# Attention weights transposed by a DMA on Sync's queue instead of by TensorE and ScalarE copies, in a two-layer hybrid decoder trunk on eight cores

## The chip, the cores and the metric

The kernel runs on the 8 NeuronCores of one Trainium2 chip. Each core has TensorE (matmuls), VectorE, ScalarE, GpSimd and SyncE, which run side by side and wait for each other on semaphores, and 16 DMA engines that all queues share. Every core computes one of the 8 sequences of the batch by itself, with the same program and the same weights; the cores exchange nothing. The metric is the device time of the slowest core in microseconds (us).

## The reference

Two layers over x of shape (8, 2048, 1024). What matters, cut down:

```python
h = rmsnorm(x, norm_mix_pre); z = h @ w_in             # u|v (gMLP), q|k|v, pool channels, 3 gates
ya, yc = gmlp_branch(...), pool_branch(...)
# differential attention, causal, 4 heads, two components of 64 each, v of 128:
sc = einsum('bqhcd,bkhcd->bhcqk', q, k) * 64**-0.5     # masked with -inf above the diagonal
p = softmax(sc)                                        # both components c = 0, 1
w = p[:, :, 0] - lam * p[:, :, 1]
out = einsum('bhqk,bkhe->bqhe', w.astype(v.dtype), v)
yb = rmsnorm(out, subln_g) * (1 - lambda_init)
merged = sum(sigmoid(gate_i) * (y_i @ w_branch_i)); x = x + rmsnorm(merged @ w_out)
x = x + rmsnorm(swiglu(rmsnorm(x)))                    # D_FF = 2816
```

The product of w with v needs w with the keys on the partitions, while the softmax leaves the queries there. So each block of 128 queries by 128 keys has to be transposed once. That transposition is what is changed.

## The kernel before

**Stages.** The work is cut into four stages: (layer 0, first half of the tokens), (layer 0, second half), (layer 1, first half), (layer 1, second half), 1024 tokens each. A stage projects K, V and Q, then runs its attention mixed in between dense matmuls: the feed-forward part of the stage before (from stage 1 on), the gMLP and pool projections, and the gates and branches `G`/`B`. Last come the 16 merge groups of branch 1 (attention's own: a gate group `ps<-HB,WS` of 8 matmuls and a branch group `ps<-QY,WS` of 4), and the output projection. Stage numbers below are 0 to 3.

**Attention's units.** One unit `u` is one head of one block of 128 queries: 32 units in a stage, `qb = u // 4` the query block, `h = u % 4` the head. A unit of an even stage has `qb + 1` = 1 to 8 key blocks, one of an odd stage `8 + qb + 1` = 9 to 16; over the four stages that is 128 units and 1088 blocks of 128x128. The keys are taken in chunks of up to 1024, so a unit of an odd stage has two chunks. For each chunk: `qk` (the score products of both components, matmuls of 64 rows, into four PSUM banks; on the last chunk the mask is added), `max` on VectorE, `exp` on ScalarE into `PB[:, u % 2, comp]`. After the last chunk: `w` (sums, reciprocals, lambda) and `wk` on VectorE, which combines the components in pieces of 512 columns, in place, into `PB[:, u % 2, 0]`. Then, in pieces of four blocks: `tr`, matmuls against the identity that put the transposed weights into a PSUM bank; `wt`, ScalarE's copy of that bank into `WT[:, rnd % 2]`; `pv`, matmuls of `WT` with `V` that accumulate into the output's bank. When the fourth head of a query block is done, `oc`, `f`, `y`, `yt`, `ye` normalize and transpose its output, and the next block's first `pv` waits for `y`. `PB` has two places: ScalarE's `exp` of unit u waits until the last `tr` of unit u - 2 has read its place.

**What sets the order.** Nothing is scheduled at run time. The class `Order` plays the program through with planned durations and writes down one fixed order for each engine; the engines then run those lists, each strictly in order. `dense` places a dense group and before it calls `run_events`, which places attention's steps (`attention_step`) if what they need is, by the plan, there. A step of `qk` also waits for its share of the dense work (`targets`). What is left of a stage's attention after the fourth merge group is placed by `finish_attention`, with no dense work in between, because the fifth group needs the last query block. The plan reckons a DMA at `mb / GBPS` plus 2.0 us, one after the other through one `dma_free` for all queues.

**Sync's queue** carries the residual loads (`xo`: 2 MB, 1.5 MB and twice 0.25 MB at each stage's merge; `xr`, 256 KB each through `NXR` places), the stores and the final output. Weights are loaded by GpSimd's queue into four slots `WS`.

## Time and profile before

| | |
|---|---|
| median of 3 runs | 2515.87 us (2510.47 to 2516.42) |
| the profiled execution's own time | 2516.2 us |
| span of its slowest core (core 0) | 2514.7 us; the cores have 2495.1 to 2514.7 us |
| mean granted TensorE clock, core 0 | 0.961 of full |
| TensorE busy (core 0) | 2289.6 us, 91% of the span |
| VectorE / ScalarE busy | 1453.5 us (58%) / 1275.8 us (51%) |
| 16 DMA engines: GpSimd's queue / Sync's queue | 38.0% / 9.6% of their time |

All rows are of core 0, the slowest. Times count from the start of its span. A busy TensorE is not TensorE at its peak, because matmuls overlap: a group's busy time divided by its count is more than one matmul costs in a run of them. PEclk is the granted clock as a share of full (1.0 is 2.4 GHz, 0.5 is 1.2 GHz).

### The profile page before, as it was taken

What the parts mean: (1) busy time and instruction counts of PE and PEld (TensorE: products, weight loads), DVE (VectorE), ACT (ScalarE), POOL (GpSimd) and SP (SyncE); (2) the same over time, 40 slices, a digit from 0 to 9 for tenths busy, and PEclk for the clock granted to TensorE, in tenths of its full rate; (3) what the DMA queues carried; (4) which work ended last, traced back from release to release, by engine and by line L of the source; (5) the groups of instructions that cost most, each with busy time, mean ns of one, the idle gap of its engine ahead of it and who ended that gap; (6) DMA issues with size and microseconds to landing.
All of it is one profiled execution on the core that took longest, in us unless ns stands there. A gap on an engine that the chain in (4) does not pass through costs nothing.

```text
span 2514.7 us, 39549 instructions; the slowest of 8 cores (2495.1 to 2514.7 us)
## 1 busy us (share of the span) xinstructions
PE 2289.6 (91%) x12332; PEld 1078.9 (43%) x12568; DVE 1453.5 (58%) x2618; ACT 1275.8 (51%) x2728; POOL 289.4 (12%) x573
## 2 busy tenths in 40 slices
PE   5999689999998997999998999999999899888996
PEld 2444344444443443444444444444444444333442
DVE  2467626777657884545524754567765778364313
ACT  2556635555675663634445542645667566442122
POOL 1111000000111100011011210001111111100011
PEclk9999789999998997999999999999999999889998
DMA  8433337333344442644346346643334533865458
GB/s 193 66 51 58 86 59 159 59 57 54 59 83 134 69 85 61 150 87 68 60 64 150 80 64 150 136 70 60 55 53 71 153 58 51 172 138 99 78 73 199
DMA packets 83369, 230.87 MB, mean 92 GB/s; under 512 B 8288, under 2 KB 9056, under 8 KB 82144
## 3 DMA queue, kind: packets, MB, share of 16 engines
q0 software_dynamic: 49456, 150.43, 38.0%
q1 hardware_dynamic: 33712, 77.91, 9.6%
q8 instruction: 108, 1.77, 0.3%
q14 instruction: 93, 0.76, 0.1%
HBM read 345.16 MB, written 33.55 MB: 151 GB/s over the span
## 4 chain that ended last, share of the span: by engine, by line
PE 81%; DMA 6%; DVE 5%; issue 4%; ACT 3%; POOL 0%; SPq 0%; another core or an unknown queue 0%; DVEq 0%; ACTq 0%; POOLq 0%
PE ps L1039 57%; PE ps L1080 11%; DMA WS<-wblk 4%; PE ps L1201 3%; PE ps L1130 2%; PE ps L1230 2%; PE ps L1215 2%; DVE st L1521 1%; DVE R L1425 1%; DMA R<-xT 1%; DVE R L1422 1%; PE ps L1205 1%; DVE TM L1425 1%; ACT WT L1283 1%; PE ps L1145 1%
## 5 line engine op out<-in xcount | busy, mean ns | idle before, releaser
L1039 PE MATMUL ps<-HB,WS 128*128 128x512 bf16 x4987 | 1165.7, 384 | 42.6 <-DMA WS<-wblk 19.8
L1039 PEld LDWEIGHTS ps<-HB,WS 128*128 128x128 bf16 x5120 | 493.2, 99 | 626.1 <-issue 88.7
L1283 ACT ACTIVATE TG<-ps 128x512 f32<-128x512 f32 x368 | 219.6, 597 | 526.2 <-PE ps L1039 518.7
L1521 DVE TENSOR_REDUCE st<-ps 128x1 f32<-128x1024 f32 (+7 forms) x384 | 343.2, 907 | 154.7 <-PE ps L1205 139.5
L1346 ACT ACTIVATE PB<-ps,st 128x1024 bf16<-128x1024 f32 (+7 forms) x384 | 331.2, 865 | 139.8 <-DVE st L1521 122.3
L1425 DVE SCALAR_TENSOR_TENSOR TM<-TG,ps 128x512 f32<-128x512 f32 x304 | 208.4, 686 | 321.1 <-PE ps L1039 169.9
L913 POOL DMA_DIRECT2D WS<-wblk x334 | 181.6, 544 | 1821.7 <-PE ps L1039 1472.0
L1080 PE MATMUL ps<-R,WS 128*128 128x512 bf16 x1371 | 313.2, 379 | 6.8 <-DMA WS<-wblk 2.9
L1283 ACT ACTIVATE R<-ps 128x512 f32<-128x512 f32 (+1 forms) x256 | 149.3, 596 | 230.9 <-PE ps L1080 108.9
L1039 PE MATMUL ps<-R,WS 128*128 128x512 bf16 x988 | 240.3, 381 | 6.6 <-DVE R L1422 1.9
L1425 DVE SCALAR_TENSOR_TENSOR PB<-PB,st 128x512 bf16<-128x512 bf16 (+3 forms) x320 | 204.4, 665 | 3.6
L1080 PEld LDWEIGHTS ps<-R,WS 128*128 128x128 bf16 x1408 | 133.7, 98 | 160.7 <-issue 13.4
L1039 PE MATMUL ps<-WS,HB 128*128 128x512 bf16 x747 | 184.2, 399 | 18.5 <-DMA WS<-wblk 14.2
L1283 ACT ACTIVATE WT<-ps 128x512 bf16<-128x512 f32 (+3 forms) x320 | 162.0, 532 | 72.5 <-PE ps L1215 71.4
L1283 ACT ACTIVATE HB<-R 128x512 bf16<-128x512 f32 x256 | 156.4, 628 | 38.4 <-DVE R L1422 18.2
L1039 PEld LDWEIGHTS ps<-R,WS 128*128 128x128 bf16 x1024 | 96.7, 98 | 115.0 <-issue 14.0
L1422 DVE TENSOR_TENSOR R<-TM,ps 128x512 bf16<-128x512 f32 x176 | 120.4, 684 | 40.1 <-PE ps L1039 36.6
L1230 PE MATMUL ps<-V,WT 128*128 128x128 bf16 x1088 | 110.1, 227 | 25.4 <-ACT WT L1283 23.3
L1215 PE MATMUL ps<-ident_s,PB 128*128 128x128 bf16 x1088 | 108.7, 225 | 22.4 <-DVE PB L1425 17.9
L1039 PEld LDWEIGHTS ps<-WS,HB 128*128 128x128 bf16 x768 | 75.7, 102 | 110.1 <-issue 37.4
L1230 PEld LDWEIGHTS ps<-V,WT 128*128 128x128 bf16 x1088 | 80.2, 101 | 74.8 <-issue 39.8
L1130 PE MATMUL ps<-HB,ones 128*128 128x512 bf16 x253 | 69.4, 421 | 46.9 <-ACT HB L1283 46.8
(90 smaller groups left out, 1708.9 us busy)
## 6 DMA issues: line engine op xcount, KB each, us to landing
WS<-wblk POOLq DMA_DIRECT2D x188, 512.0 KB, 5.5
WS<-wblk POOLq DMA_DIRECT2D x74, 352.0 KB, 4.6
xm<-R SPq DMA_DIRECT2D x8, 2048.0 KB, 9.5
XR<-xm SPq DMA_DIRECT2D x64, 256.0 KB, 6.3
WS<-wblk POOLq DMA_DIRECT2D x40, 384.0 KB, 5.6
R<-xT SPq DMA_DIRECT2D x16, 512.0 KB, 12.2
WS<-wblk POOLq DMA_DIRECT2D x32, 256.0 KB, 6.6
x<-R SPq DMA_DIRECT2D x4, 2048.0 KB, 10.7
```

The source lines that it names most:

```text
L913: e.dma_start(out=WS[:, m % NSLOT, 0:n], in_=src).then_inc(*inc(f"WS{m % NSLOT}", block, 16))
L1039: mm = e.matmul(bank(b), lh, rh, start=i == 0, stop=i == len(pairs) - 1)
L1080: mm = e.matmul(bank(C.bank[key]), w[:, k, :], aT[:, part * 11 + k, tile_of(t)], start=part == 0 and k == 0, stop=part == 1 and k == 10)
L1130: mm = e.matmul(bank(C.bank[key]), ones[:], h_buffer(kind, s)[:, c, tile_of(t)], start=c == 0, stop=c == 7)
L1201: mm = e.matmul(ps[:, 2 * comp + b, 0:m], QY[cs, h, qb * 128:(qb + 1) * 128], KT[cs, h, first + 512 * p:first + 512 * p + m], start=True, ...
L1215: mm = e.matmul(ps[:, C.bank[key], (k % 4) * 128:(k % 4 + 1) * 128], PB[:, u % 2, 0, k * 128:(k + 1) * 128], ident[:], start=True, stop=True)
L1230: mm = e.matmul(ps[:, O_BANK, h * 128:(h + 1) * 128], WT[:, rnd % 2, (k % 4) * 128:(k % 4 + 1) * 128], V[:, k, h * 128:(h + 1) * 128], sta ...
L1283: e.activation(out=out, in_=in_, func=func, scale=scale, bias=bias).then_inc(*inc(sem, key))
L1346: e.activation(out=PB[:, par, comp, first:first + n], in_=src, func=AF.Exp, bias=st[:, par, nm + comp:nm + comp + 1], scale=1.0, accum_out ...
L1422: e.tensor_tensor(out=out, in0=in0, in1=in1, op=op).then_inc(*inc(sem, key))
L1425: e.scalar_tensor_tensor(out=out, in0=in0, scalar=scalar, in1=in1, op0=op0, op1=op1).then_inc(*inc(sem, key))
L1521: e.tensor_reduce(out=col(2 if c else 0), in_=src, axis=AX.X, op=ALU.max, negate=True).then_inc(*inc("dve_max", (s, u, c, comp, "m") if c ...
```

## The change

The transposition moves off TensorE. `tr` and `wt`, the buffer `WT` and their semaphores are gone. When all `wk` of a unit are done, Sync issues one DMA, `tp`, that transposes all blocks of the unit from `PB[:, u % 2, 0]` into `PB[:, u % 2, 1]`, the second component's place, which the combination has read by then. `pv` reads its stationary operand from there, in pieces of eight blocks instead of four. ScalarE's `exp` of unit u now waits for the last `pv` of unit u - 2. The plan gives the DMA 0.04 MB a block, so 0.14 us a block after whatever its `dma_free` holds, and 2.0 us. The space of `WT` goes to a fourth place of `XR` (`NXR`).

```diff
-NXR = 3
+NXR = 4
@@ Order.attention_step
-        if a["tr"] and len(a["pv"]) < 2 and self.there([a["tr"][0][0]], True):
-            self.tr()
-            return True
@@ Order.qk, after the last chunk
-            for r in range(0, nblk, 4):
-                nb = min(4, nblk - r)
-                p = self.op("dve", ("wk", s, u, r // 4), 0.12 + 0.128 * nb, 2, [w])
-                a["tr"].append((p, u, r // 4, nb, r + 4 >= nblk))
-
-    def tr(self):
...
-        self.item(label, 0.07 * nb, [need], wt)
-        if last:
-            self.happened(("taken", a["s"], u), self.now)
-        self.op("act", wt, 0.15 + 0.115 * nb, 0, [("pe", label)])
...
+            p = [self.op("dve", ("wk", s, u, r), 0.12 + 0.128 * min(4, nblk - 4 * r), 2, [w]) for r in range((nblk + 3) // 4)]
+            t = self.op("sp", ("tp", s, u), 0.1, 0, p, mb=nblk * 0.04)
+            for r in range(0, nblk, 8):
+                a["pv"].append((t, u, r, min(8, nblk - r), r + 8 >= nblk))
@@ Order.pv
+        if last:
+            self.happened(("taken", s, u), self.now)
@@ build_program
-    WT = sb("WT", [128, 2, 512], BF16)
@@ sp_program
+        def tp(s, u):
+
+            par = u % 2
+            n = (STAGES[s][1] * 8 + u // 4 + 1) * 128
+            p.wait_ge(*ev("dve_w", (s, u, (n - 1) // 512)))
+            e.dma_start_transpose(out=PB[:, par, 1, 0:n].rearrange("p (k q) -> p k q", q=128), in_=PB[:, par, 0, 0:n]).then_inc(
+                *inc(f"TP{par}", (s, u), 16))
@@ pe_program
-        def tr(s, u, r, rnd):
...
-            for k in range(4 * r, min(4 * r + 4, nblk)):
-                mm = e.matmul(ps[:, C.bank[key], (k % 4) * 128:(k % 4 + 1) * 128], PB[:, u % 2, 0, k * 128:(k + 1) * 128], ident[:],
-                              start=True, stop=True)
-            mm.then_inc(*inc("pe_tr", (s, u, r)))
-        def pv(s, u, r, rnd):
+        def pv(s, u, part):
...
-            pe.wait_ge(*ev("act_wt", (s, u, r)))
-            for k in range(4 * r, min(4 * r + 4, nblk)):
+            pe.wait_ge(*ev(f"TP{par}", (s, u)))
+            for k in range(8 * part, min(8 * part + 8, nblk)):
...
-                mm = e.matmul(ps[:, O_BANK, h * 128:(h + 1) * 128], WT[:, rnd % 2, (k % 4) * 128:(k % 4 + 1) * 128],
+                mm = e.matmul(ps[:, O_BANK, h * 128:(h + 1) * 128], PB[:, par, 1, k * 128:(k + 1) * 128],
                               V[:, k, h * 128:(h + 1) * 128], start=k == 0, stop=k == nblk - 1)
@@ act_program, exp
-                a.wait_ge(*ev("pe_tr", (s if u >= 2 else s - 1, u - 2 if u >= 2 else 30 + u, (H * 8 + qb) // 4)))
+                a.wait_ge(*ev("pe_pv", (s if u >= 2 else s - 1, u - 2 if u >= 2 else 30 + u, (H * 8 + qb) // 8)))
```

**How the order moves on TensorE.** `Order` makes a new order for every engine. The place that matters is the stretch between the fourth merge group and the fifth, the tail that `finish_attention` writes. First TensorE in stage 1 before, from the fourth group's branch (`ps<-QY,WS`) on. L1201 `ps<-KT,QY 128x512 x4` is one chunk of 1024 keys, L1205 its mask, L1215 the transpositions, L1230 the products with V, L1241 the transposed output `yt`.

```order
971 L1039 MATMUL ps<-QY,WS 128x512 x4
972 L1215 MATMUL ps<-ident_s,PB 128x128 x8
973 L1201 MATMUL ps<-KT,QY 128x512 x4
974 L1205 MATMUL ps<-mask_s,ident_s 128x128 x2
975 L1230 MATMUL ps<-V,WT 128x128 x4
...
985 L1230 MATMUL ps<-V,WT 128x128 x8
986 L1241 MATMUL ps<-ident_s,YB 128x128 x4
987 L1039 MATMUL ps<-HB,WS 128x512 x8
```

The same stretch of the changed kernel, where the lines are L1197 (score products), L1201 (mask), L1216 (products with V, which now read `PB`) and L1227 (`yt`).

```order
764 L1035 MATMUL ps<-QY,WS 128x512 x4
765 L1197 MATMUL ps<-KT,QY 128x512 x4
766 L1216 MATMUL ps<-V,PB 128x128 x15
767 L1197 MATMUL ps<-KT,QY 128x512 x4
768 L1201 MATMUL ps<-mask_s,ident_s 128x128 x2
...
773 L1201 MATMUL ps<-mask_s,ident_s 128x128 x2
774 L1216 MATMUL ps<-V,PB 128x128 x16
775 L1197 MATMUL ps<-KT,QY 128x512 x8
776 L1201 MATMUL ps<-mask_s,ident_s 128x128 x2
777 L1216 MATMUL ps<-V,PB 128x128 x16
778 L1197 MATMUL ps<-KT,QY 128x512 x8
```

The tail of stage 1 holds one chunk of score products before and eight (four units) in the changed kernel. Counted in the same way over the whole order: stage 0 has 5 units (of one chunk) in its tail before and 13 now; stage 2 none in both; stage 3 none before and 7 chunks (of four units) now. Together 6 before, 28 now.

**Sync's queue.** Here are the changed kernel's rows around stage 0's residual loads (R and XR from xT), where before there were only the loads and the stores. L992 is `tp`, and the middle number is its count of blocks.

```order
9 L992 DMA_TRANSPOSE PB<-PB 128x3x128 x4
10 L992 DMA_TRANSPOSE PB<-PB 128x4x128 x4
11 L979 DMA R<-xT 128x4096
12 L981 DMA R<-xT 128x3072
13 L985 DMA XR<-xT 128x512 x2
14 L992 DMA_TRANSPOSE PB<-PB 128x5x128 x4
15 L992 DMA_TRANSPOSE PB<-PB 128x6x128 x4
16 L992 DMA_TRANSPOSE PB<-PB 128x7x128 x4
17 L992 DMA_TRANSPOSE PB<-PB 128x8x128 x4
18 L998 DMA xm<-R 1024x1x512 x2
```

The 16 transpositions of stage 0's last four query blocks now stand in the same queue behind 4 MB of residual loads.

## Rows read from the trace of the kernel before

**Rows 1.** The page's head: span and each engine's busy time.

```profile
span 2514.7 us, 39549 instructions; the slowest of 8 cores (2495.1 to 2514.7 us)
PE 2289.6 (91%) x12332; PEld 1078.9 (43%) x12568; DVE 1453.5 (58%) x2618; ACT 1275.8 (51%) x2728; POOL 289.4 (12%) x573
```

**Rows 2.** The chain that ended last, shares of the span by engine.

```profile
PE 81%; DMA 6%; DVE 5%; issue 4%; ACT 3%; POOL 0%; SPq 0%; another core or an unknown queue 0%; DVEq 0%; ACTq 0%; POOLq 0%
```

**Rows 3.** Groups by line: busy us, mean ns of one, idle before them and its releasers.

```profile
L1283 ACT ACTIVATE WT<-ps 128x512 bf16<-128x512 f32 (+3 forms) x320 | 162.0, 532 | 72.5 <-PE ps L1215 71.4
L1230 PE MATMUL ps<-V,WT 128*128 128x128 bf16 x1088 | 110.1, 227 | 25.4 <-ACT WT L1283 23.3
L1215 PE MATMUL ps<-ident_s,PB 128*128 128x128 bf16 x1088 | 108.7, 225 | 22.4 <-DVE PB L1425 17.9 <-DVE TM L1425 1.6 <-DVE R L1425 1.2
```

**Rows 4.** Stretches: length, busy us of each engine, PEclk, DMA share, GB/s.

```profile
36.00:260.00 224.00, 214.26 (x1182) 101.26 (x1204) 130.91 (x268) 123.10 (x303) 33.22 (x68) 0.98 0.43 72
281.00:325.00 44.00, 21.96 (x159) 12.74 (x159) 24.14 (x38) 27.32 (x67) 4.28 (x10) 0.62 0.01 1
388.00:927.00 539.00, 508.31 (x2965) 244.40 (x3021) 387.60 (x729) 330.00 (x719) 61.63 (x120) 0.99 0.43 81
949.00:976.00 27.00, 12.31 (x81) 7.49 (x81) 11.74 (x21) 12.69 (x32) 1.81 (x5) 0.56 0.00 1
1038.00:1516.00 478.00, 462.23 (x2444) 217.65 (x2491) 259.17 (x449) 227.37 (x501) 62.19 (x121) 0.99 0.48 90
1595.00:2136.00 541.00, 513.80 (x3026) 248.31 (x3082) 391.05 (x738) 327.71 (x719) 58.22 (x116) 0.98 0.42 80
2154.00:2162.00 8.00, 2.62 (x10) 1.00 (x9) 1.38 (x2) 2.73 (x14) 2.79 (x6) 0.71 0.97 164
```

**Rows 5.** Waits in 281 to 325, in 949 to 976, then of the whole span.

```profile
PE ps L1215 <- DVE PB L1425: 9.8, 6, 2.5
...
PE ps L1215 <- DVE PB L1425: 8.1, 2, 4.4
...
DVE R L1422 <- DMA XR<-xm: 27.9, 13, 7.0
```

**Rows 6.** Timeline of stage 1's tail: start, duration, engine, line; idle in brackets.

```profile
956.00 1.03 PE L1201 MATMUL ps<-KT,QY 64*128 64x512 bf16 x4
...
962.08 0.30 ACT L1283 ACTIVATE st<-st 128x1 f32<-128x1 f32 x1
...
964.06 2.74 DVE L1425 SCALAR_TENSOR_TENSOR PB<-PB,st 128x512 bf16<-128x512 bf16 x4
...
969.20 0.59 PE L1230 MATMUL ps<-V,WT 128*128 128x128 bf16 x4 [0.27 <-ACT WT L1283]
...
975.11 0.34 PEld L1241 LDWEIGHTS ps<-ident_s,YB 128*128 128x128 bf16 x4 [5.59 <-issue]
```

**Rows 7.** Timeline of stage 0's merge and tail, in the same columns.

```profile
260.67 0.50 PE L1230 MATMUL ps<-V,WT 128*128 128x128 bf16 x6
...
289.98 1.04 PE L1201 MATMUL ps<-KT,QY 64*128 64x512 bf16 x4
...
295.40 0.96 PE L1201 MATMUL ps<-KT,QY 64*128 64x512 bf16 x4
...
296.49 0.95 PE L1230 MATMUL ps<-V,WT 128*128 128x128 bf16 x7
296.80 2.36 DVE L1521 TENSOR_REDUCE st<-ps 128x1 f32<-128x1024 f32 x2 [1.04 <-PE ps L1205]
```

**Rows 8.** DMA issues: count, KB each, median us from issue to landing.

```profile
WS<-wblk POOLq DMA_DIRECT2D x188, 512.0 KB, 5.5
...
R<-xT SPq DMA_DIRECT2D x16, 512.0 KB, 12.2
...
R<-xT SPq DMA_DIRECT2D x2, 2048.0 KB, 15.9
...
cols_s<-cols SPq DMA_DIRECT2D x1, 40.0 KB, 2.4
```

More of the change, by code:

```diff
@@ L137, in dma_start, with dma_start_transpose @@
     def dma_start(self, *a, **k):
+        return self
+    def dma_start_transpose(self, *a, **k):
         return self
@@ L413, in attention @@
             cum += x
-        self.att = {"s": s, "qk": qk, "targets": targets, "i": 0, "bank": [None, None], "alt": 0, "tr": [], "pv": [],
-                    "round": 0, "start": self.progress}
+        self.att = {"s": s, "qk": qk, "targets": targets, "i": 0, "bank": [None, None], "alt": 0, "pv": [], "start": self.progress}
     def qk_needs(self):
@@ L490, in pv @@
         needs = self.pv_needs()
-        need, u, r, nb, last, rnd = a["pv"].pop(0)
-        label = ("pv", s, u, r, rnd)
+        need, u, r, nb, last = a["pv"].pop(0)
+        label = ("pv", s, u, r // 8)
         qb = u // 4
         self.item(label, 0.07 * nb, needs)
+        if last:
+            self.happened(("taken", s, u), self.now)
         if last and u % 4 == 3:
@@ L504, in finish_attention @@
         a["targets"] = [0.0 for x in a["targets"]]
-        while a["i"] < len(a["qk"]) or a["tr"] or a["pv"] or any(e[0][0] == "yt" for e in self.events):
+        while a["i"] < len(a["qk"]) or a["pv"] or any(e[0][0] == "yt" for e in self.events):
             self.run_events()
@@ L1017, in sp_program @@
         e.dma_start(out=cols[:], in_=colsd).then_inc(*inc("COLS", 0, 16))
-        work = {"x0": x0, "xr": xr, "xo": xo, "store": store, "out": out, "gbc": gbc_load}
+        work = {"x0": x0, "xr": xr, "xo": xo, "tp": tp, "store": store, "out": out, "gbc": gbc_load}
         for n, (name, *args) in enumerate(order["sp"]):
@@ L1206, in qk @@
             mm.then_inc(*inc("pe_qk", (s, u, c)))
-        def tr(s, u, r, rnd):
-            nblk = STAGES[s][1] * 8 + u // 4 + 1
-            key = ("tr", s, u, r)
-            C.take(key)
-            pe.wait_ge(*ev("dve_w", (s, u, r)))
-            pe.wait_ge(*C.free(key))
-            for k in range(4 * r, min(4 * r + 4, nblk)):
-                mm = e.matmul(ps[:, C.bank[key], (k % 4) * 128:(k % 4 + 1) * 128], PB[:, u % 2, 0, k * 128:(k + 1) * 128], ident[:],
-                              start=True, stop=True)
-            mm.then_inc(*inc("pe_tr", (s, u, r)))
-        def pv(s, u, r, rnd):
+        def pv(s, u, part):
             H, qb, h = STAGES[s][1], u // 4, u % 4
             nblk = H * 8 + qb + 1
+            par = u % 2
             key = ("O", s, qb)
-            if h == 0 and r == 0:
+            if h == 0 and part == 0:
                 C.take(key, bank=O_BANK)
                 pe.wait_ge(*C.free(key))
-            pe.wait_ge(*ev("act_wt", (s, u, r)))
-            for k in range(4 * r, min(4 * r + 4, nblk)):
+            pe.wait_ge(*ev(f"TP{par}", (s, u)))
+            for k in range(8 * part, min(8 * part + 8, nblk)):
                 vkey = ("V", s - 1 if H and k < 8 else s, k % 8)
                 pe.wait_ge(*ev(plan.evac[vkey], vkey))
-                mm = e.matmul(ps[:, O_BANK, h * 128:(h + 1) * 128], WT[:, rnd % 2, (k % 4) * 128:(k % 4 + 1) * 128],
+                mm = e.matmul(ps[:, O_BANK, h * 128:(h + 1) * 128], PB[:, par, 1, k * 128:(k + 1) * 128],
                               V[:, k, h * 128:(h + 1) * 128], start=k == 0, stop=k == nblk - 1)
-            mm.then_inc(*inc("pe_pv", (s, u, r)))
+            mm.then_inc(*inc("pe_pv", (s, u, part)))
         def yt(s, qb):
@@ L1352, in exp @@
                     st[:, par, 4 + comp:5 + comp])
[L1354 to L1361 removed]
         def oc(s, qb):
[L1365 removed]
+            a.wait_ge(*ev("pe_pv", (s, qb * 4 + 3, (STAGES[s][1] * 8 + qb) // 8)))
             if qb or s:
@@ L1399, in gelu @@
             C.frees(key, "act_gelu", key)
-        work = {"ev": evac, "th": th, "sc": sc, "sq": sq, "sqx": sqx, "rs": rs, "exp": exp, "wt": wt, "oc": oc, "y": y, "ye": ye, "gelu": gelu}
+        work = {"ev": evac, "th": th, "sc": sc, "sq": sq, "sqx": sqx, "rs": rs, "exp": exp, "oc": oc, "y": y, "ye": ye, "gelu": gelu}
         a.wait_ge(*ev("dve_const", "sub"))
@@ L1409, in act_program @@
             work[name](*args)
-    rounds = [label[1:4] for label in plan.pe if label[0] == "tr"]
-    round_of = {k: i for i, k in enumerate(rounds)}
-    def two_before(s, u, r):
-        return rounds[round_of[s, u, r] - 2]
     def dve_program(e):
```

25 lines of the change are left out of this document (5 added, 20 removed).

## The prediction

> **What bounds the kernel now.** I read the page's head first: TensorE is busy in 91% of the span [rows 1], and the chain that ended last lies to 81% on it [rows 2]. So what is taken from TensorE in the dense stretches is worth its full time. Next the stretches [rows 4]. In the four long ones (36 to 260, 388 to 927, 1038 to 1516, 1595 to 2136) TensorE is busy for 1698.6 of 1782 us, 95%, at a granted clock of 0.98 to 0.99. It is idle for 83 us of them. The three short ones are the tails, where attention runs alone because the fifth merge group waits for it: 281 to 325, 949 to 976 and 2154 to 2162. There TensorE is busy in 22.0 of 44 us, 12.3 of 27 and 2.6 of 8, and its clock is granted at 0.62, 0.56 and 0.71, that is, mostly at the lower of its two levels after it had been idle. A tail is set by the chain from score product to weights to output, not by TensorE's work. These two regimes pull the change apart: it takes work from TensorE where TensorE is the limit, and it makes the chain longer where the chain is the limit.
>
> **What is removed.** (a) 1088 transposing matmuls [rows 3]. Their mean of 225 ns is not their price, since they overlap: six matmuls of this shape in a run take 0.50 us from the first start to the last end [rows 7], so (0.50 - 0.23) / 5 = 55 ns each. In the tails stand about a third of their 159 + 81 matmuls, 80 [rows 4], which don't count. 1008 x 55 ns = 55 us. (b) TensorE's waits before them and before the products with V: 22.4 + 25.4 us [rows 3], of which 9.8 + 8.1 are in the tails [rows 5], leaves 30 us in the dense stretches. (c) ScalarE's 320 copies, 162 us [rows 3]. ScalarE is not the limit, but the dense stretches have 83 - 30 = 53 us of other idle time, and a quarter of it is a fair guess for what a less loaded ScalarE gives back: 13 us. (d) Attention that leaves the dense stretches for the tails: 28 - 6 = 22 chunks. A chunk costs TensorE about 0.6 us of score products and mask at the full clock (1.03 for the products alone at the lower one, [rows 6], half of it at the full one) and eight products with V, 8 x 55 ns = 0.44: 22 x 1.05 = 23 us. Sum: 55 + 30 + 13 + 23 = 121 us off the dense stretches. The fourth place of XR can take little: VectorE waits 27.9 us for those loads [rows 5], and nearly all of that lies beside feed-forward and projection matmuls. I take 3 us, so 124.
>
> **What is added.** 128 DMAs on Sync's queue, 34 MB. The trace has no transposing DMA and no copy from SBUF to SBUF. Bounds for the longest (16 blocks, 512 KB): below, 2.4 us, the landing of the smallest load; above, 12.2 us, the 512 KB loads of x, which start in a crowd. The nearest row is the 512 KB weight load, 5.5 us [rows 8]. I take that for 16 blocks, and (2.4 + 5.5) / 2 = 4 us for eight. The order gives a transposition about 0.14 us a block plus 2 us before it places the products with V, 4.3 us for 16 blocks. In the dense stretches those products stand behind other dense groups, so a landing that is a microsecond late is mostly covered by them.
>
> The Trainium skill has two figures that disagree here. "VectorE: DVE Perf Modes", section "The three transpose paths", gives a 128x128 block 390 ns on TensorE and 1309 ns by DMA, and its rules send a transposition to TensorE where PSUM will do. The trace doesn't bear out the first as a cost in a run (55 ns). "DMA: Bandwidth & Descriptors", in "Latency and other measured facts", gives a DMA transpose 261 GB/s, by which 16 blocks would need 2 us beside the fixed part, and the landing would be near 4 us. By that the sum below would be about 10 us smaller.
>
> **The tails.** This is the term that decides. The order has 6 chunks of score products between the fourth and the fifth merge group before, and 28 now. Attention falls behind because a place of PB is now held through the DMA and up to the last product with V, where before the transposing matmul freed it.
>
> Stage 1: one chunk before, four units of two chunks now. From a chunk's score products to the end of its exponentials is 956.0 to 962.1, 6.1 us; from there to the end of the combination (964.06 + 2.74 = 966.8) is 4.7 us [rows 6]. The maxima and the combinations share VectorE and the chunks share the four score banks, so I let little overlap: a unit is 2 x 6.1 + 4.7 = 16.9 us, four are 68. Behind the last come its landing, 5.5, its 16 products at the lower clock, 1.8 (seven take 0.95 us there, so (0.95 - 0.28) / 6 = 0.11 each [rows 7]), and the output's normalization up to its transposition, 969.8 to 975.1 [rows 6], 5.3: 12.6 us. Sum 80 us against 27 now: +53. Stage 3: 3.5 units and the same end, 59 + 12.6 = 72, against 8: +64. Stage 0: 13 units of one chunk instead of 5. Now a unit follows the other after 5.4 us (289.98 to 295.40 [rows 7]). With the DMA the path of one unit is the products, 1.0, the maxima, 2.4 [rows 7], 3.3 of the last exponential, weights and combination (an estimate from the 4.7 us that follow a two-chunk unit's exponentials [rows 6], with half the blocks), 4 of landing and 0.95 of products with V [rows 7], 11.7 us; two places share it, 5.8 us a unit. 13 x 5.8 = 75, plus the three changes of query block, whose first product with V waits for the normalization of the one before (5.3 us each, [rows 6]), 16 us: 91 against 44, +47. The first transpositions also stand behind 4 MB of residual loads whose 2 MB part lands after 15.9 us [rows 8]; TensorE waits there for weights anyway, so I add nothing. Stage 2 has no tail before or after. Sum of the tails: 53 + 64 + 47 = 164 us.
>
> **The sum.** 2516.2 (the profiled execution, span 2514.7) - 124 + 164 = 2556 us. The profiled execution is 0.3 us above the median of the runs, so the forecast is 2555 us, 1.6% slower.
>
> **The rivals.** *The main case*, landings of 3 to 6.5 us for 16 blocks, tails as priced: 2528 to 2595. Chance 0.68.
>
> *Late landings.* If 16 blocks land only after 8 us or more, the products with V stand at the head of TensorE's queue and stop the dense work. Being in order, everything behind them waits. The 64 two-chunk units are about 3.7 us later than the order gives them; 1 to 2 us of it covered leaves 2 us a unit, 128 us less what the tails already hold: some 2640. For it speaks that there is no row of such a DMA and that these DMAs share 16 engines that are 41 to 48% busy [rows 4]; against it, that the large weight loads land in 5.5 us in that very traffic. Chance 0.14. *Block by block:* each 32 KB block handled as a small DMA, one after the other, at 2.4 us [rows 8]. A mean unit of 8.5 blocks would land after 20 us, 17 beyond what the order gives, 128 times: +2180 us, 4700 in all. The skill's 1309 ns a block, by its page on VectorE, would be this rival at half the price. Against it: a 40 KB and a 512 KB transfer differ by 3 us and not by a factor of 13 [rows 8]. Chance 0.03.
>
> *Faster.* If in the tails VectorE alone is the limit (the next unit's first chunk slips in beside the DMA of the one before), a two-chunk unit costs its share of VectorE: four maxima of 1.2 us, 4 x 0.69 of combination [rows 6, 7] and some 2.5 us of small ones, 10 us instead of 16.9. The tails then add 25 + 40 + 25 = 90 us, and 2516 - 124 + 90 = 2482. It decides for the other sign as soon as a two-chunk unit costs less than about 12 us. For it: VectorE is busy in only 11.7 of 27 us of that tail now [rows 4]. Against it: both chunks of a unit need all four score banks, and the order stands fixed. Chance 0.07. *No change:* the two sums, 124 and 164, each off by a fifth in opposite directions: 2508 to 2523. Chance 0.08.
>
> **How the numbers follow.** About 0.3% (8 us) is what a measurement of this kernel can tell from no change. Slower by more: 0.68 + 0.14 + 0.03, so 0.85; within: 0.08; faster: 0.07. The range cuts most of the faster case and the far part of late landings: 2520 to 2625 us. The likeliest case's own range is 2528 to 2595.
>
> **What the profile after would show.** No copies into WT; 128 DMA issues PB<-PB on Sync's queue, 16 blocks landing in 4 to 6 us; TensorE's products with V at the same 227 ns and half as many groups. The 124 us off the dense stretches, shared out by blocks (400 of 1088 in each odd stage, 144 in each even one): about 46 us less from stage 1's first K to its last `B` of branch 2, the same in stage 3, 16 in stages 0 and 2. The tails near 91, 80 and 72 us, at a granted clock of 0.5 to 0.6, with the wait for PB<-PB and ScalarE's `exp` on the chain there. I am wrong if TensorE waits for PB<-PB by more than some 40 us outside the tails (late landings), or if the tails are under 60 us each (faster).

## The result and the profile after

The changed kernel takes 2587.0 and 2587.5 us, the kernel before beside it 2510.5 to 2516.4. The ratio is 1.029, with a 95% interval of 1.026 to 1.032: slower by 2.9%. The forecast was 2555 us, slower by 1.6%, with a range of 2520 to 2625. Sign and range hold; of the two terms one was too large by 37 us, and the place where that was lost is the subject below. (In this and the other comparisons executions in which one die ran disturbed, here one of 2786.9 us, are left out, so a median of all runs can be higher than the ratio says.)

The page of the changed kernel: its head, the granted clock (tenths in 40 slices), the queues (packets, MB, share of the 16 engines), and the chain that ended last by engine and by line.

```profile
span 2585.4 us, 36541 instructions; the slowest of 8 cores (2565.9 to 2585.4 us)
PE 2253.3 (87%) x11480; PEld 1021.3 (40%) x11480; DVE 1459.6 (56%) x2620; ACT 1144.5 (44%) x2414; POOL 288.1 (11%) x573
PEclk8999579999998985999999999999999997698998
q0 software_dynamic: 49456, 150.43, 37.5%
q1 hardware_dynamic: 177072, 113.57, 17.9%
PE 70%; DMA 14%; DVE 7%; ACT 4%; issue 3%; SPq 1%; POOL 1%; DVEq 0%; ACTq 0%; POOLq 0%
PE ps L1035 52%; DMA PB<-PB 8%; PE ps L1076 8%; DMA WS<-wblk 3%; PE ps L1197 3%; PE ps L1216 3%; DMA XR<-xm 2%; DVE PB L1396 2%; DVE st L1492 2%; PE ps L1126 2%; ACT PB L1332 1%; DVE R L1396 1%; DMA R<-xT 1%; PE ps L1201 1%; DVE R L1393 1%
```

TensorE is busy for 36 us less than in [rows 1] and yet the span is 71 us longer. Its share of the chain fell from 81% [rows 2] to 70%; the DMAs' rose from 6% to 14%, and 8 points of that are the transposition itself. ScalarE has 131 us less to do, and its share of the chain is 4% where it was 3%, so that did not shorten the chain.

The groups that answer to [rows 3], and the stretches that answer to [rows 4]: the four dense ones, the three tails.

```profile
L1216 PE MATMUL ps<-V,PB 128*128 128x128 bf16 x1088 | 99.2, 248 | 102.3 <-DMA PB<-PB 102.1
L1197 PE MATMUL ps<-KT,QY 64*128 64x512 bf16 (+3 forms) x640 | 102.8, 386 | 75.2 <-ACT PB L1332 75.2
```

```profile
37.00:245.00 208.00, 201.29 (x1034) 91.91 (x1033) 109.06 (x221) 95.15 (x218) 29.19 (x57) 0.98 0.50 83
416.00:929.00 513.00, 482.07 (x2567) 219.46 (x2565) 360.70 (x675) 264.91 (x569) 58.75 (x115) 0.97 0.60 104
1084.00:1563.00 479.00, 459.67 (x2344) 208.81 (x2343) 260.33 (x450) 205.70 (x451) 62.01 (x121) 0.98 0.54 100
1643.00:2145.00 502.00, 479.98 (x2577) 218.25 (x2576) 356.05 (x672) 267.79 (x568) 56.60 (x111) 0.98 0.59 106
266.00:355.00 89.00, 32.73 (x210) 16.15 (x209) 50.57 (x86) 40.09 (x109) 8.34 (x20) 0.53 0.22 39
945.00:1021.00 76.00, 24.45 (x150) 12.91 (x149) 42.79 (x80) 28.41 (x73) 3.61 (x10) 0.54 0.23 47
2169.00:2233.00 64.00, 20.35 (x133) 11.30 (x132) 35.34 (x66) 23.86 (x63) 4.14 (x11) 0.55 0.40 77
```

The dense stretches have shrunk and the tails have grown, as foretold, and little else moved: what lies between them (`merge` below) takes 6 us more, the rest, with the output projections, the same. The one core of the page hides some of this, for the cores differ by up to 20 us, so the table below gives each sum as the mean over the eight cores of the profiled execution. "Dense" runs from a stage's first K matmul to its last `B` of branch 2, "merge" from there to the fourth merge group, "tail" from the fourth to the fifth, each summed over the four stages; the moments are start times of those groups in the traces. "Wait" is TensorE's wait before the products with V on the slowest core (where TensorE transposes, its wait before that comes on top, 22.4 us in [rows 3]).

| kernel | dense | merge | tails | rest | sum | wait |
|---|---|---|---|---|---|---|
| before | 1772.6 | 76.9 | 77.4 | 577.4 | 2504.3 | 25.4 |
| changed | 1685.5 | 83.4 | 229.3 | 576.9 | 2575.1 | 102.3 |
| no transposition, order of the changed | 1647.8 | 81.1 | 199.9 | 578.4 | 2507.2 | 18.7 |
| no transposition, own order | 1677.2 | 78.3 | 170.8 | 575.6 | 2501.8 | 45.6 |
| copy, long pieces | 1656.4 | 82.5 | 219.9 | 576.8 | 2535.6 | 54.0 |
| copy, 254-byte pieces | 1664.6 | 81.1 | 226.0 | 575.3 | 2547.0 | 71.1 |
| before, place held longer | 1769.7 | 76.9 | 109.4 | 575.2 | 2531.2 | 25.1 |
| landing planned apart | 1742.8 | 108.6 | 175.7 | 575.4 | 2602.5 | 136.9 |
| early place, RESERVE 100 | 1681.5 | 76.9 | 209.2 | 574.3 | 2541.9 | 106.4 |
| changed, half maxima | 1699.4 | 82.4 | 132.8 | 574.8 | 2489.4 | 75.5 |
| before, half maxima | 1792.8 | 75.0 | 31.7 | 574.1 | 2473.7 | 17.8 |
| copy, half maxima | 1681.8 | 82.9 | 123.2 | 575.2 | 2463.0 | 36.2 |
| before, RESERVE 100 | 1777.2 | 76.4 | 57.0 | 574.7 | 2485.4 | 22.6 |
| before, half maxima, RESERVE 100 | 1777.5 | 75.6 | 31.7 | 574.8 | 2459.7 | 13.9 |

Each row is one execution. The mean over the cores of all executions of a kernel lies within 8 us of its sum here, so a difference of less than that between two rows says little.

Where TensorE waits for the transposition: first in the dense stretch of stage 1, then in stage 3's merge, then in the tails of stages 1, 0 and 3 (us in all, times, longest).

```profile
PE ps L1216 <- DMA PB<-PB: 21.8, 7, 13.5
PE ps L1216 <- DMA PB<-PB: 9.5, 1, 9.5
PE ps L1216 <- DMA PB<-PB: 24.1, 6, 7.2
PE ps L1216 <- DMA PB<-PB: 13.6, 9, 5.8
PE ps L1216 <- DMA PB<-PB: 19.3, 4, 7.2
```

With 0.2, 5.9 and 7.6 us in the other dense stretches that is 45 us outside the tails and 57 in them, on the slowest core; the mean over the cores is 33 and 60. Sync's line of the transposition (duration in ns on its sequencer, min/median/max, and the landing), and the worst one:

```profile
L992 SPq DMA_TRANSPOSE PB<-PB x128: 1079/1334/10198, 83.4 to 2220.4; - x128
DMA to landing us min/median/max: 2.2/4.3/22.4
...
L992 SPq DMA_TRANSPOSE PB<-PB x1: 6337/6337/6337, 818.5 to 818.5; - x1
...
841.01 1.65 PE L1216 MATMUL ps<-V,PB 128*128 128x128 bf16 x14 [13.54 <-DMA PB<-PB]
...
L901 POOL DMA_DIRECT2D WS<-wblk x2: 560/570/579, 818.9 to 819.5; - x2
...
DMA to landing us min/median/max: 21.7/22.1/22.4
```

Fourteen blocks issued at 818.5 us land 22.4 us later, with no residual load of Sync's queue open; the next unit's fourteen blocks land in 4.0. TensorE stands for 13.5 us, with all dense work queued behind that product. The last two lines are the two weight loads that GpSimd issued right behind it: they took 21.7 and 22.4 us as well. At this place of the program that happened on four of the eight cores (17.6 to 22.4 us). On the other four, and on all eight cores of the kernel before, of the one without a transposition and of both copies below, those two loads landed in 5.9 to 9.5 us.

### The profile page after: what moved, and what is told of

Read it like the earlier page. It is cut to its first block, busy times and chain, and to the rows that moved or that the text cites. A ratio compares the mean times of both kernels' runs of the same rounds, so it can differ in the third digit from the quotient of the medians.

```text
span 2585.4 us, 36541 instructions; the slowest of 8 cores (2565.9 to 2585.4 us)
## 1 busy us (share of the span) xinstructions
PE 2253.3 (87%) x11480; PEld 1021.3 (40%) x11480; DVE 1459.6 (56%) x2620; ACT 1144.5 (44%) x2414; POOL 288.1 (11%) x573
## 4 chain that ended last, share of the span: by engine, by line
PE 70%; DMA 14%; DVE 7%; ACT 4%; issue 3%; SPq 1%; POOL 1%; DVEq 0%; ACTq 0%; POOLq 0%
PE ps L1035 52%; DMA PB<-PB 8%; PE ps L1076 8%; DMA WS<-wblk 3%; PE ps L1197 3%; PE ps L1216 3%; DMA XR<-xm 2%; DVE PB L1396 2%; DVE st L1492 2%; PE ps L1126 2%; ACT PB L1332 1%; DVE R L1396 1%; DMA R<-xT 1%; PE ps L1201 1%; DVE R L1393 1%
## 5 line engine op out<-in xcount | busy, mean ns | idle before, releaser
L1035 PE MATMUL ps<-HB,WS 128*128 128x512 bf16 x5120 | 1180.4, 384 | 23.1 <-DMA WS<-wblk 10.0
L1076 PE MATMUL ps<-R,WS 128*128 128x512 bf16 x1408 | 314.2, 380 | 4.0 <-DMA WS<-wblk 3.8
L1035 PE MATMUL ps<-R,WS 128*128 128x512 bf16 x1024 | 245.1, 381 | 2.3 <-DVE R L1393 1.9
L1216 PE MATMUL ps<-V,PB 128*128 128x128 bf16 x1088 | 99.2, 248 | 102.3 <-DMA PB<-PB 102.1
L1197 PE MATMUL ps<-KT,QY 64*128 64x512 bf16 (+3 forms) x640 | 102.8, 386 | 75.2 <-ACT PB L1332 75.2
L1216 PEld LDWEIGHTS ps<-V,PB 128*128 128x128 bf16 x1088 | 82.6, 112 | 134.7 <-issue 120.3
L1035 PEld LDWEIGHTS ps<-WS,HB 128*128 128x128 bf16 x768 | 75.5, 101 | 95.2 <-issue 18.9
```

Source lines behind the costliest of these rows:

```text
L1035: mm = e.matmul(bank(b), lh, rh, start=i == 0, stop=i == len(pairs) - 1)
L1076: mm = e.matmul(bank(C.bank[key]), w[:, k, :], aT[:, part * 11 + k, tile_of(t)], start=part == 0 and k == 0, stop=part == 1 and k == 10)
L1197: mm = e.matmul(ps[:, 2 * comp + b, 0:m], QY[cs, h, qb * 128:(qb + 1) * 128], KT[cs, h, first + 512 * p:first + 512 * p + m], start=True, ...
L1216: mm = e.matmul(ps[:, O_BANK, h * 128:(h + 1) * 128], PB[:, par, 1, k * 128:(k + 1) * 128], V[:, k, h * 128:(h + 1) * 128], start=k == 0, ...
```

## The experiments

**The transposition left out.** `none_same` keeps the changed kernel's order, has no transposing DMA, and reads the weights as they lie; `none_replan` lets the plan know of it.

```diff
-            e.dma_start_transpose(out=PB[:, par, 1, 0:n]..., in_=PB[:, par, 0, 0:n]).then_inc(
-            pe.wait_ge(*ev(f"TP{par}", (s, u)))
+            pe.wait_ge(*ev("dve_w", (s, u, (nblk - 1) // 4)))
@@ none_replan, the plan too
-            t = self.op("sp", ("tp", s, u), 0.1, 0, p, mb=nblk * 0.04)
+            t = p[-1]
```

> The changed kernel without any transposition: Sync's DMA is left out and the products with V read the combined weights as they are (so the attention output is computed from untransposed weights). The order on TensorE, VectorE and ScalarE is word for word that of the changed kernel. Theory landing (the DMA's landing, in the tails and in weight traffic, is what was under-priced): TensorE's 30 us of waits for it in the dense stretches go, and each tail loses 2 to 4 us a unit, some 60 us in all: 2587 - 90 = about 2500 us. Rival order (the tails exist because the order puts 28 chunks there, and the chain there is the exponentials and VectorE): the tails stay above 160 of their 226 us, and the time stays above 2530 us.

> As before without any transposition (untransposed weights are multiplied with V), but the plan knows it: no DMA in its reckoning, so it makes an order of its own. This is the most that taking the transposition off TensorE and ScalarE could ever give. Theory held place (attention falls behind because its place is held through the DMA): with no DMA attention keeps pace, tails near the 79 us of before, time 2516 - 110 = about 2405 us. Rival own pace (attention is limited by its own chain of maxima, exponentials and combination; TensorE's transpositions were time in which that chain went on anyway, and without them less time passes per dense group, so more is left over for the tails): tails of 150 us or more, time about 2440 to 2465 us. The order it makes has 10, 7, 0 and 5 chunks in the tails of stages 0 to 3, which speaks for the rival.

Measured: ratio 1.0093 (1.0062 to 1.0125) in the same order, 1.0046 (1.0002 to 1.0090) in its own. In the same order the dense stretches lose 38 us against the changed kernel and the tails 29: that is the price of the DMA. The theory 'landing' had 60 for the tails. The rest of them, 200 us, is the order's, as the rival had it. With the plan told, the tails still hold 22 chunks (10, 7, 0 and 5, counted in the order) and 171 us: the dense stretches are 95 us shorter than before, the tails 93 longer. So a transposition that costs nothing at all would have gained nothing, in the two orders tried. Both expectations had a gain there, 2405 or 2440 to 2465 us; the tails above 150 us came as the second had them, and that they take back everything was the surprise. Both orders are written with `RESERVE` 24. A larger one gives the kernel before 0.6% (below), and no run tries it without the transposition, so an order that keeps some of the gain isn't ruled out.

**Only the longer hold.** `hold` is the kernel before, with the place of `PB` freed by the last `pv` instead of the last `tr`.

```diff
-                a.wait_ge(*ev("pe_tr", (s if u >= 2 else s - 1, u - 2 if u >= 2 else 30 + u, (H * 8 + qb) // 4)))
+                a.wait_ge(*ev("pe_pv", (s if u >= 2 else s - 1, u - 2 if u >= 2 else 30 + u, (H * 8 + qb) // 4)))
```

> The kernel before, TensorE still transposing, with one part of the change alone: the place in PB is freed by the last product with V instead of by the last transposition, in the plan and in ScalarE's wait. Theory held place: attention falls behind in every stage, some half of the 147 us of added tail comes, 2570 us. Rival own pace: only stage 0 (no feed-forward work beside it) gets a longer tail, its order has 10 chunks there instead of 5, the others are as before: 2516 + 25 = about 2540 us.

Measured: 1.0126 (1.0066 to 1.0186), from two executions. Only stage 0's tail grew, from 43 to 75 us; those of stages 1 and 3 stayed at 26 and 7. The hold explains 32 of the 45 us that stage 0's tail gained and nothing of the 108 us of the two odd stages' tails.

**The plan told of the true landing.** `plan_own` reckons a transposition at 2.1 us plus 0.14 a block, apart from the line of the other DMAs.

```diff
+        if label[0] == "tp":
+            end += 2.1 + mb / self.GBPS
-        if mb:
+        elif mb:
```

> The changed kernel with another reckoning in the plan alone: a transposition takes 2.1 us and 0.14 us a block from its issue and no longer stands behind weight and residual loads in the plan's one DMA line. These are the landings measured in quiet stretches. Theory plan (the plan's DMA line made attention look late and pushed it into the tails): 19 chunks in the tails instead of 28, most of stage 3's tail gone, 2587 - 45 = about 2542 us. Rival landing (in weight traffic a transposition really lands after 6 to 22 us, so an order that trusts 4.3 us makes TensorE wait in the dense stretches): waits for PB<-PB outside the tails grow from 30 us to 80 or more and the time stays above 2570 us.

Measured: 1.0449 (1.0368 to 1.0530), the slowest of all. The quiet landing is right where it is quiet. But with the products with V placed that early, each late landing stops dense work, as the rival said: 137 us of waits, dense stretches 57 us longer than the changed kernel's, the way from them to the fourth merge group 25 longer, tails 54 shorter.

```profile
L1218 PE MATMUL ps<-V,PB 128*128 128x128 bf16 x1088 | 96.0, 242 | 136.9 <-DMA PB<-PB 136.8
```

**A copy in place of the transposition.** The same bytes from the same place to the same place: `copy` in rows of up to 4 KB, `copy256` in pieces of 254 bytes.

```diff
-            e.dma_start_transpose(out=PB[:, par, 1, 0:n]..., in_=PB[:, par, 0, 0:n]).then_inc(
+            e.dma_start(out=PB[:, par, 1, 0:n], in_=PB[:, par, 0, 0:n]).then_inc(
@@ copy256
+            v = lambda c: PB[:, par, c, 0:n].rearrange("p (k q) -> p k q", q=128)[:, :, 0:127]
+            e.dma_start(out=v(1), in_=v(0)).then_inc(
```

> The changed kernel with its 128 transposing DMAs replaced by plain DMA copies of the same bytes between the same places, at the same points of Sync's queue, waited for in the same way (the output is not the reference's, since nothing transposes the weights). Theory 'small packets': a transposing DMA is cut into packets of some 250 bytes, and each of them stands behind a weight packet of 3 KB, so it is its packets that land late (up to 22 us) beside weight loads; a copy of the same bytes in rows of 2 to 4 KB has a tenth of the packets, and lands in under 6 us nearly everywhere. TensorE's waits for PB<-PB fall from 102 us to under 50, and the time comes near that of the kernel without any transposition in the same order: 2535 to 2555 us. Rival 'traffic': the 16 engines are simply full at these places, and whatever stands in Sync's queue is late: landings over 10 us stay as frequent, the waits stay at 90 to 110 us, and the time at 2575 to 2600.

> As the plain copy in place of the transposition, but cut by hand into short pieces: of each block of 128 columns the first 127 are copied, so that a piece is 254 bytes, as the transposition's packets are, and can't be joined to its neighbour (the output is not the reference's: nothing transposes, and one column of each block is left out). It asks whether it is the shortness of the packets or the transposing itself that costs the 2.4 to 3 us between a transposition and a copy of 14 to 16 blocks and the 48 us between their kernels (2588 and 2540). Theory 'small packets': landings of 4 to 5 us for 16 blocks in quiet, some over 10 beside weight loads without a residual load being open, waits for PB<-PB of 85 to 110 us, time 2570 to 2595. Rival 'transposing': landings as in the plain copy (2.9 us for 16 blocks), waits of 50 to 60 us, time 2535 to 2550.

Measured: 1.0112 (1.0091 to 1.0133) and 1.0145 (1.0058 to 1.0231). The packets of all queues together, in the changed kernel, with the long copy (with its line and landings, as above) and with the short copy:

```profile
DMA packets 226715, 266.34 MB, mean 103 GB/s; under 512 B 151648, under 2 KB 152416, under 8 KB 225504
```

```profile
DMA packets 101787, 266.33 MB, mean 105 GB/s; under 512 B 11360, under 2 KB 18272, under 8 KB 100576
L992 SPq DMA_DIRECT2D PB<-PB x128: 464/465/931, 81.8 to 2177.6; - x128
DMA to landing us min/median/max: 1.7/2.9/19.7
```

```profile
DMA packets 224667, 266.05 MB, mean 105 GB/s; under 512 B 149600, under 2 KB 150368, under 8 KB 223456
```

The long copy's time, 2537 to 2544 us, came out as the first theory said, 45 us under the transposition by the ratios; the wait halved, to 54 us, just above the 50 of that theory. But its reason is only part of it. In the profiles' means the three kernels stand at 2575, 2547 and 2536 us. Cutting the copy short costs 11 us and gives it the transposition's slope with the blocks: sixteen blocks land in 4.1 us in quiet (2.9 in long rows, 4.3 transposed). The other 28 us go with the transposing itself: on core 0, the same core in all three, the waits are 94.0, 70.8 and 55.7 us. By the ratios alone the short copy is faster than the transposition but can't be told from the long copy (its interval takes in the long copy's whole interval). The mean over the cores of all executions does tell the three apart: 2571 and 2575 us transposed, 2539 to 2555 in short pieces, 2524 to 2536 in long ones. The wait of 71 us lies between the two expectations, and of the four times, 2544 to 2576 us, two lie in the range of the first and two at that of the second, so neither theory holds alone. Of the 28 us, 21 lie in the dense stretches, where TensorE waits 23.6 us for the landing in the mean of the cores, against 7.7 with the short copy and 4.4 with the long one. Why a transposition lands later there than a copy in equally short packets is not settled. A transposition holds Sync's sequencer for a median of 1.33 us where a copy holds it for 0.46, and up to 10.2 on the slowest core, and 6 to 9 transpositions in 128 land after more than 10 us, against 3 to 5 long copies. The long copies that landed after 12 us or more, up to 20, were all issued behind open transfers of Sync's own queue. The 22.4 us transposition above was not, and there the weight loads beside it were late too, which at that place happened beside no copy.

**VectorE's maxima halved.** Each maximum is taken over the first half of its chunk's columns, in the changed kernel (`aft_half`) and in the one before (`bef_half`), and the plan knows. In both the softmax stays what it was, as the maximum only shifts the exponent, as long as no score of the other half exceeds it so far that the exponential overflows.

```diff
-            src = ps[...].rearrange("p a b -> p (a b)")[:, 0:n]
+            src = ps[...].rearrange("p a b -> p (a b)")[:, 0:n // 2]
@@ the plan
-            m = self.op("dve", ("max", s, u, c, comp), 0.2 + 1.0e-3 * n + (0.3 if c else 0.0), 1, [("pe", label)])
+            m = self.op("dve", ("max", s, u, c, comp), 0.2 + 0.5e-3 * n + (0.3 if c else 0.0), 1, [("pe", label)])
```

> The changed kernel in which each maximum of the scores is taken over the first half of its columns alone (the other half is left out, so the output is not the reference's), and the plan that makes the order knows of the lower price; the exponentials, combinations and transpositions stay. It takes about 0.4 us from each of 384 instructions on VectorE (907 ns now), 150 us in all, and nothing from TensorE. Theory 'own pace': attention is paced by its own chain, in which VectorE's maxima and combinations are the longest part, so with the transpositions gone from TensorE the dense work ran ahead of it. With cheaper maxima the order leaves nothing to the tails of stages 1 and 3 (8 and 7 chunks now); these tails fall from 75 + 63 to about 25 + 30 us, and the time from 2588 to 2505 to 2535 us. Rival 'places': the two places of PB and the four score banks with the DMA's landing set the pace, and VectorE has room: the tails fall by less than 30 us in sum, and the time stays above 2555.

> The control: the same edit (maxima over the first half of the columns, the output not the reference's) in the kernel before, with its plan knowing of it. TensorE is the limit there in 95% of the dense stretches and only 6 chunks are in the tails, so 'own pace' expects little: the tails of 79 us fall by 20 to 40, the dense stretches by under 20, time 2470 to 2505 us, that is, a gain of less than half of what the same edit gives the changed kernel. If the gain is as large as there, VectorE is as much a limit before as after, and the change did not shift the bound.

Measured: 0.9952 (0.9937 to 0.9967) and 0.9907 (0.9886 to 0.9928), against the kernel before in both cases. From the maxima

```profile
L1492 DVE TENSOR_REDUCE st<-ps 128x1 f32<-128x1024 f32 (+7 forms) x384 | 343.1, 907 | 212.4 <-PE ps L1201 179.2
```

to their halves

```profile
L1492 DVE TENSOR_REDUCE st<-ps 128x1 f32<-128x512 f32 (+7 forms) x384 | 195.7, 530 | 205.8 <-PE ps L1201 181.5
```

VectorE is relieved of some 147 us in each kernel, and TensorE of nothing. The changed kernel gains 86 us in the table, the one before 31. The tails of stages 1 and 3 fall from 75 and 66 to 20 and 23 us, as expected, and stage 0's stays at 89. (The time, 2499 us, came out below the 2505 to 2535 expected.) So the change made VectorE's share of attention, which was nearly covered before, into a limit. It is still the slower of the two with the maxima halved, by 16 us of means. The edit shortens the maxima and changes the order at once, and no run separates these two effects.

**Both costs away at once.** `copy_half` is the long copy with halved maxima.

> The two costs taken away together: the changed kernel with plain copies in place of the transposing DMAs, and with the maxima over the first half of the columns, in the plan for those (the output is not the reference's, nothing transposes). Theory: the transposing matmuls' 80 us in the dense stretches are worth having only where attention's own pace has room. With the maxima halved the changed kernel took 2499 and the one before 2490; the copy takes 45 us more off, so 2445 to 2470, some 1.5% faster than the kernel before with the same maxima: the change's idea would have paid there with a DMA that lands like a copy. Rival: the tails and the waits that are left (stage 0's 90 us above all) keep it at 2480 or more, so that there would be nothing to win even so.

Measured: 0.9841 (0.9786 to 0.9896), 2479 to 2489 us, above the 2445 to 2470 of the theory, where the kernel before beside it had 2507 to 2533. In the means it stands at 2463 us against 2474 of `bef_half`, but the two ratios' intervals touch, and `bef_half_R100` below, which keeps the transposition on TensorE, has 0.9834. Whether the idea would have won there stays open; the 123 us of tails that are left, 84 of them stage 0's on the profiled core, are what holds it.

**Attempts at a better kernel.** `early_R100` frees the first component's half of a place when the transposition has landed, and keeps more work back for attention's end. `bef_R100` is the kernel before with that second edit alone, `bef_half_R100` has the halved maxima as well.

```diff
-RESERVE = 24.0
+RESERVE = 100.0
@@ early_R100, the plan (the exp's wait in the same way)
-            taken = [("taken", s, u - 2)] if u >= 2 and c == 0 else []
+            taken = [("taken" if comp else "tp", s, u - 2)] if u >= 2 and c == 0 else []
```

> The changed kernel with two edits that aim at the tails: the first component's half of a place of PB may be written as soon as its transposition has landed (the second half still waits for the last product with V), and the work kept back for attention's end is larger (RESERVE 100 in place of 24), which leaves 9, 6, 0 and 7 chunks in the tails where there were 13, 8, 0 and 7. Theory 'places': being held up to the last product with V is what paces attention; the tails of stages 0 and 1 fall by 20 and 15 us and the time by 30 to 45, to 2540 to 2560 us. Theory 'own pace': the exponentials wait for VectorE's maxima anyway, only the shift of chunks counts, and the time is 2565 to 2590 us. Neither expects it to beat the kernel before.

> The kernel before with more work kept back for attention's end in the plan (RESERVE 100 in place of 24), which leaves 2, 1, 0 and 0 chunks of score products in the tails where there were 5, 1, 0 and 0. By 'own pace' a chunk in stage 0's tail costs about 7 us and one in the dense stretch 1: the tail of 43 us falls to some 25, the time by 5 to 15 us, to 2497 to 2508. Rival: the held work only moves and the dense stretch grows by as much: 2508 to 2516.

> The kernel before with both edits that may beat it: maxima over the first half of the columns of each chunk (a maximum only shifts the exponent, so the weights stay the same ratio unless a score in the other half exceeds it by a great deal) and RESERVE 100. With halved maxima alone it took 2490. The plan's tails are the same with and without the larger RESERVE (2, 0, 0, 0 chunks), so the expected gain on 2490 is small: 2480 to 2492 us. If it comes out at 2470 or below, the place of the held work matters beyond the tails.

Measured: 1.0207 (1.0169 to 1.0245), 0.9935 (0.9893 to 0.9978) and 0.9834 (0.9707 to 0.9961). The first lies between its two expectations, at 2563 us: stages 0 and 1 gave 15 us each, and stage 3's tail took 10 back. The second does what was expected, stage 0's tail from 43 to 23 us, and beats the kernel before by 0.6% with nothing of the mathematics touched. The third is the fastest that kept the transposition on TensorE, 2466 and 2467 us in two executions and 2498 in another, with an interval too wide to rank it against halved maxima alone or to choose between its expectations.

## Why the prediction was right, and what was mis-sized

**TensorE's side, 124 us off the dense stretches: measured 87 (78 between the two profiled cores).** By stage it is 15, 35, 3 and 34 us, where the prediction had 16, 46, 16 and 46. The terms (a) to (d) were right in sum: without the DMA the same order gives 125. By parts they were not, and that the sum came out is luck. In the mean over the cores the waits of (b) gave 23 us, priced at 30; the other idle time fell from 43.6 us to 41.8, so (c), 13 us, was 2; and TensorE's busy time fell by 100 us, where (a) and (d) had 78. What failed is the landing, priced at 5.5 us wherever it falls, and with it the sentence "a landing that is a microsecond late is mostly covered": of the seven waits in stage 1's dense stretch one is 13.5 us and the other six are 1.4 us in the mean. In quiet the step was right, 2.1 us plus 0.14 a block, 4.3 for sixteen against my 5.5. In the traffic of weight loads it was 5 to 22 us, and I had priced this as a rival of 0.14 and put nothing of it into the sum. It cost the dense stretches 38 us in the mean, 24 of them TensorE's waits for the landing itself. My own sign of being wrong was more than some 40 us of waits outside the tails, and the slowest core has 45 (33 in the mean of the cores): on that core the main case failed by its own sign. The rival came true in kind, at under half of its price (38 us, where its 2640 stands 85 above the forecast), because few landings were late and not all.

**The tails, +164 us: measured +152 (147).** By stage 45, 49 and 59 us in the means, against 47, 53 and 64. Two of the parts were wrong and made up for each other, which again is luck. The units of stage 1's tail follow each other faster than the 16.9 us priced:

```profile
984.00 1.11 ACT L1332 ACTIVATE PB<-ps,st 128x1024 bf16<-128x1024 f32 x1
985.34 1.04 PE L1197 MATMUL ps<-KT,QY 64*128 64x512 bf16 x4 [3.93 <-ACT PB L1332]
991.34 1.87 PE L1216 MATMUL ps<-V,PB 128*128 128x128 bf16 x16 [4.63 <-DMA PB<-PB]
993.14 1.04 PE L1197 MATMUL ps<-KT,QY 64*128 64x512 bf16 x4
994.28 2.35 DVE L1492 TENSOR_REDUCE st<-ps 128x1 f32<-128x1024 f32 x2 [1.51 <-PE ps L1197]
996.55 2.73 DVE L1396 SCALAR_TENSOR_TENSOR PB<-PB,st 128x512 bf16<-128x512 bf16 x4
1003.80 1.87 PE L1216 MATMUL ps<-V,PB 128*128 128x128 bf16 x16 [4.34 <-DMA PB<-PB]
1012.89 1.87 PE L1216 MATMUL ps<-V,PB 128*128 128x128 bf16 x16 [7.23 <-DMA PB<-PB]
```

From 991.34 to 1003.80 is 12.5 us, a ring: products with V 1.8, the scores of the next unit but one 1.1, its maxima 2.3, the combination of the unit in between 2.7 that stands behind them on VectorE, and 4.5 from its end, at 999.3, to the landing. So the "faster" case's overlap of two units is there, but the DMA is a link of the ring: with the plain copy, which lands 1.4 us sooner, this tail is 5 us shorter (70 against 75 in the mean of the cores), and without any DMA 10. The products of the four units begin at 978.6, 991.3, 1003.8 and 1012.9, 34 us where three times 16.9 would be 51. That is 11.4 us a unit, under the 12 at which the prediction let the sign turn. The sign held because of what I had left out, the start: the tail begins with a unit that is not through yet, and the first of the four reaches its products 33 us in, not the 16.9 + 5.5 us priced. The end, 7.6 us from the last products on, is as priced (1.8 + 5.3).

**The reason given for the tails was wrong.** The prediction says that attention falls behind because a place of `PB` is held longer. `hold` shows that this is a reason in stage 0 alone. In stages 1 and 3 it falls behind with no DMA at all, and catches up when the maxima are halved. Attention's chain through VectorE and ScalarE has a pace of its own; the transposing matmuls took TensorE's time while that chain went on, and when they are taken away the dense groups run out sooner and what is left is done alone, at a granted clock of 0.53 to 0.55. I had counted the order's chunks rightly and so the sum was right; the cause I gave would have sent a reader to enlarge `PB`, for which `hold` speaks in stage 0 alone. (`early_R100`, which frees half a place sooner, took 15 us off the tails of stages 0 and 1 each, but it moves chunks out of them as well.)

**The other rivals.** *Block by block* is refuted by 2.1 us plus 0.14 a block. The Trainium skill, "VectorE: DVE Perf Modes", section "The three transpose paths", gives one block 1309 ns by DMA; as a price of each block of a longer DMA the trace does not agree with it (0.14 us). The Trainium skill's 261 GB/s ("DMA: Bandwidth & Descriptors", "Latency and other measured facts") would be 0.13 us a block, an estimate from that figure, and with that the quiet landings agree. *Faster* and *no change* did not come; even the kernel without a transposition reached only no change. **The hidden parts:** XR's fourth place is not told apart by any run; the rest hardly moved, and the way to the fourth merge group took 6 us more. **Readings of the prediction that were off, without weight:** the 16 engines are 42 to 48% busy in [rows 4], not 41; of the waits in (b) another 3 us, before the products with V, lie in the tails; and 2.4 us is the shortest landing, of 40 KB, while smaller loads took longer.

**Sum:** 2516 - 78 + 147 + 3 of merge - 2 of the rest = 2586 us, against 2587 measured. Of the 71 us in the means, 67 are the DMA's price (38 dense, 29 in tails) and about 3 the exchange of TensorE's work for tails. These are single executions. The mean over the cores of all executions gives 61 and 10, and the ratios, which go by the slowest core, 50 and 23: the DMA is the larger part in all three, but its size is known only to within some 20 us.

## What to carry to other kernels

Work that is taken from the limiting engine is worth its time only as long as the chain beside it can keep the shorter pace: before such a change, count what a unit of the other chain costs its own busiest engine and where the units go that no longer fit. Here a DMA put between two compute steps of an in-order engine had to be priced by its landing in the heaviest traffic of its place, not in quiet, and the consumer placed by that. An experiment that leaves the new operation out altogether, in both orders, shows in two runs what it could give at most in those orders; here it was nothing.

## What the runs showed of the hardware

- A transposing DMA from SBUF to SBUF lands in 2.1 us plus 0.14 us per 128x128 block of bf16 in quiet (2.2, 3.0 and 4.3 us for 1, 8 and 16), a plain copy of the same bytes in 1.6 plus 0.08 (2.9 for 16), in pieces of 254 bytes 1.6 plus 0.16 (4.1). The 128 of them add 143,360 packets to Sync's queue, 35.7 MB, some 250 bytes each.
- Beside weight loads of 512 KB the same transpositions land in 5 to 22 us, and at one place two weight loads issued right behind one took 18 to 22 us on four of eight cores, where they take 6 to 9.5 beside a plain copy or nothing. Behind open residual loads of 2 and 1.5 MB one transposition took 31 us in `aft_half` and one 34 us in `early_R100`.
- They hold Sync's sequencer for 1.1 us (one block) to 1.9 us (sixteen) each in quiet, and up to 11.7 in traffic; a plain copy 0.5.
- Six products of 128x128 blocks in a run cost TensorE 55 ns each [rows 7], and 1088 transposing ones of that shape with their waits and copies are, in this kernel, worth no measurable gain: leaving them out gave a ratio of 1.0046.
- Halving the columns of a maximum over PSUM took it from 907 to 530 ns in the mean.
